# Even layer of a two-layer decoder step: six projections first, from split operands, then one run of attention steps

## The reference, cut to what matters

```python
proj = xn @ w_in                       # 1024 -> 6 x 512: q, k, v, g_a, u, g_b
z = q @ k.T / 8 + bias                 # per head, 8 heads of 64
lneg = where(mask, log_sigmoid(-z), 0)
tail = reverse_cumsum(lneg) - lneg     # stick-breaking weights
o_a = where(mask, exp(log_sigmoid(z) + tail), 0) @ v
o_b = pool_mix(u)                      # causal window means of 2, 4, 8, 16 and a small matmul
mixed = concat(o_a * silu(g_a), o_b * silu(g_b))
h = h + mixed @ w_out                  # k and v are outputs, too
```

## Time and profile before

| | |
|---|---|
| three runs, us | 2433.32, 2422.24, 2419.28 (median 2422.24) |
| the profiled execution, device time | 2424.9 us |
| its span in the trace | 2423.1 us |
| mean granted TensorE clock | 0.936 of 2.4 GHz |
| even layer up to the end of decode attention | 854.6 us of the span |

### The profile page before, as it was taken

The page is one execution under the profiler, slowest core; times in us unless marked ns, Lnnn a source line. Parts: engine busy times, 40 slices in busy tenths (PEclk is TensorE's granted clock), DMA queues, the critical chain, the costliest instruction groups (busy, mean ns, idle before and its releaser), DMA issues. The chain is left out here.

```text
span 2423.1 us, 28102 instructions
## 1 busy us (share of the span) xinstructions
PE 2126.3 (88%) x10945; PEld 1552.5 (64%) x10945; DVE 1072.6 (44%) x1840; ACT 650.8 (27%) x1116; POOL 94.4 (4%) x149
## 2 busy tenths in 40 slices
PE   4979797968967589899999979989999999967998
PEld 3646464644433234599999968559569569546885
DVE  4060606060222112274434345675675685656442
ACT  4150606060002111142222232132133133124321
POOL 0000000000000000000000000110110110110000
PEclk8989898989989699899999988899999999988999
DMA  3010101006026461258569432452453451756561
GB/s 119 14 40 6 47 0 53 0 24 190 21 85 200 134 166 63 41 107 130 143 155 188 133 136 83 170 182 93 170 193 112 177 191 61 262 191 205 156 178 31
DMA packets 180321, 281.81 MB, mean 116 GB/s; under 512 B 15363, under 2 KB 114695, under 8 KB 179098
## 3 DMA queue, kind: packets, MB, share of 16 engines
q1 hardware_dynamic: 151093, 183.12, 28.1%
q0 software_dynamic: 24256, 88.82, 10.2%
q10 hardware_dynamic: 4864, 8.39, 1.1%
HBM read 185.17 MB, written 95.31 MB: 116 GB/s over the span
## 5 line engine op out<-in xcount | busy, mean ns | idle before, releaser
L1297 PE MATMUL pre_ps<-x_xh,pre_wh 128*128 128x358 f32 (+1 forms) x792 | 260.3, 329 | 7.0 <-DVE pre_wl L1419 7.0
L1298 PE MATMUL pre_ps<-norm_xl,pre_wh 128*128 128x358 f32 (+1 forms) x792 | 259.1, 327 | 0.0
L1299 PE MATMUL pre_ps<-x_xh,pre_wl 128*128 128x358 f32 (+1 forms) x792 | 258.8, 327 | 0.0
L393 PE MATMUL attn_ps<-x_xnT,attn_w 128*128 128x512 f32 (+1 forms) x576 | 193.4, 498 | 9.5 <-DMA attn_w<-in_w_in_a 7.6
L393 PEld LDWEIGHTS attn_ps<-x_xnT,attn_w 128*128 128x128 f32 x576 | 97.0, 194 | 105.8 <-issue 98.1
L1297 PEld LDWEIGHTS pre_ps<-x_xh,pre_wh 128*128 128x128 f32 x792 | 149.8, 189 | 8.5 <-DVE pre_wl L1419 7.5
L1299 PEld LDWEIGHTS pre_ps<-x_xh,pre_wl 128*128 128x128 f32 x792 | 149.8, 189 | 0.0
L1298 PEld LDWEIGHTS pre_ps<-norm_xl,pre_wh 128*128 128x128 f32 x792 | 149.7, 189 | 0.0
L653 PE MATMUL pool_ps<-x_xnT,pool_w 128*128 128x512 f32 (+1 forms) x384 | 131.0, 504 | 13.9 <-DMA pool_w<-in_w_in_a 8.9
L1725 PE MATMUL head_ps<-head_cl,head_wh 128*128 128x358 f32 (+1 forms) x384 | 125.3, 326 | 0.0
L1724 PE MATMUL head_ps<-head_ch,head_wh 128*128 128x358 f32 (+1 forms) x384 | 125.0, 325 | 0.0
(11 more groups left out here) (388 smaller groups left out, 3795.6 us busy)
## 6 DMA issues: line engine op xcount, KB each, us to landing
head_Cs<-in_state_C POOLq DMA_DIRECT2D x32, 1024.0 KB, 5.8
out_C_s<-head_Cs POOLq DMA_DIRECT2D x32, 1024.0 KB, 4.8
x_xnT<-in_cache_sb_k SPq DMA_DIRECT2D x64, 256.0 KB, 3.0
all_w<-in_w_in_c SPq DMA_DIRECT2D x32, 512.0 KB, 10.7
x_dram<-low_low SPq DMA_DIRECT2D x16, 536.0 KB, 8.7
ca_dram<-low_low SPq DMA_DIRECT2D x16, 536.0 KB, 12.3
b_dram<-low_mid SPq DMA_DIRECT2D x16, 536.0 KB, 5.6
a_dram<-low_low SPq DMA_DIRECT2D x16, 536.0 KB, 6.1
```

The source lines that it names most:

```text
L393: last = pe.matmul(ps[:, bank + c, 0:c1 - c0], w[:, u, k, :], xnT[:, k, c0:c1], start=(k == 0), stop=(k == KD - 1))
L1297: pe.matmul(out, wh[:, t % 2, k, :], xh[:, k, c0:c1], start=(k == 0), stop=False)
L1298: pe.matmul(out, wh[:, t % 2, k, :], xl[:, k, c0:c1], start=False, stop=False)
L1299: last = pe.matmul(out, wl[:, t % 2, k, :], xh[:, k, c0:c1], start=False, stop=(k == KD - 1))
```

## The change

The even layer is cut in another way. `load_constants` also loads the first four token blocks, three weight blocks and the page table. `norm0_stage` leaves the normalised input as a high part `xe` and a low part `xl`. `even_input` makes all projections in one block: 24 weight blocks of 128 columns in the order of `TILES`, three products each, chunks of 368 columns. The means' small matmul (`y`) stands behind some of them (`TURNS`). v is made like k, features on partitions, and both are turned to token rows on PE (`turn_tokens`) through two PSUM banks (`side`). q, k and v of all heads stay in SBUF; the gates are written into `mixT` and later multiplied in place. `attention_steps` is one unrolled sequence of 36 groups, pair 0 rising from `t` = 0 to 8, pair 1 falling, and so on; the weights overwrite the sigmoid (`pos`), and the 16 columns of the longest rows beyond 1024 go through `tail`. SP loads the first four key units and the first sequence's values during these steps; values of the next three sequences are loaded within `decode_attention`.

```diff
+TILES = [("u", 0), ("u", 1), ("b", 0), ("u", 2), ("b", 1), ("u", 3), ("b", 2), ("b", 3)]
+TILES += [("v", c) for c in range(PAIRS)]
+TILES += [(kind, p) for p in range(PAIRS) for kind in "kqa"]
+AFTER = {("b", 0): 0, ("b", 1): 1, ("b", 2): 2, ("v", 0): 3}
...
+            def project(n):
+                t = tile_of(*TURNS[n])
+                pe.wait_ge(wl_done, t + 1)
+                wait_banks(n)
+                for c, (c0, c1) in enumerate(ECH):
+                    out = chunk(3 * (n % 2), c)
+                    for k in range(KD):
+                        pe.matmul(out, wh[:, t % 2, k, :], xh[:, k, c0:c1], start=(k == 0), stop=False)
+                        pe.matmul(out, wh[:, t % 2, k, :], xl[:, k, c0:c1], start=False, stop=False)
+                        last = pe.matmul(out, wl[:, t % 2, k, :], xh[:, k, c0:c1], start=False, stop=(k == KD - 1))
+                last.then_inc(full, 1)
...
+            def wait_side(r):
+                if r < 2:
+                    pe.wait_ge(rows_done, 2)
+                else:
+                    pe.wait_ge(side_done, r - 1)
...
+                    for c in range(PAIRS):
+                        if t == tile_of("v", c) + 1:
+                            for g in range(3):
+                                turn_tokens("v", c, g)
+                    if kind == "q":
+                        turn_tokens("k", p, 0)
+                        turn_tokens("k", p, 1)
+                    elif kind == "a":
+                        turn_tokens("k", p, 2)
...
+            def high(t):
+                act.wait_ge(w_in[t % WR], 16 * (t // WR + 1))
+                if t >= 2:
+                    act.wait_ge(full, turn_of(*TILES[t - 2]) + 1)
+                act.activation(wh[:, t % 2], w[:, t % WR], ACT.Copy).then_inc(wh_done, 1)
...
+            high(0)
+            for t in range(NF):
+                if t + 1 < NF:
+                    high(t + 1)
+                save(t)
...
+            for t, (kind, p) in enumerate(TILES):
+                if t + 1 < NF:
+                    low(t + 1)
...
+                for c in range(PAIRS):
+                    if t == tile_of("v", c) + 2:
+                        save_values(c)
...
+    GROUPS = [(p, t) for p in range(PAIRS) for t in (range(NT + 1) if p % 2 == 0 else range(NT, -1, -1))]
...
+            for n in range(KS):
+                load_pages(sp, table, cache_k, n // 2, PAGES // 2 * (n % 2), PAGES // 2, kp[:, n], k_in[n])
+            load_pages(sp, table, cache_v, 0, 0, PAGES, vp0, v_in0)
...
+            for u, (b, f) in enumerate(units[KS:], KS):
+                sp.wait_ge(z_full, u - KS + 1)
                 load_pages(sp, table, cache_k, b, HALF * f, HALF, kp[:, u % KS], k_in[u % KS])
+                if u % 2 == 0 and u < KS + 2 * (BG - 1):
+                    bb = (u - KS) // 2 + 1
+                    load_pages(sp, table, cache_v, bb, 0, PAGES, vp[bb], v_in[bb])
```

More of the change, by code:

```diff
@@ L150, in sem, with load_constants @@
         return self.sems[-1]
-def load_constants(nc, d, const, half, vcol, wcol, bias, prefT):
+def load_constants(nc, d, const, half, vcol, wcol, bias, biasN, prefT, x, x_in, w, w_in, table):
     with ExitStack() as ctx:
@@ L175, in _ @@
             sp.dma_start(prow[:, :], d["state_pool"].rearrange("l b r c -> (l b r) c")).then_inc(landed, 16)
+            sp.dma_start(table[:, :], d["page_table"].rearrange("(o b) n -> o (b n)", o=1)).then_inc(landed, 16)
+            for i in range(1, XS):
+                sp.dma_start(x[:, i, :], x_rows[i]).then_inc(x_in[i], 16)
+            for t in range(WR):
+                load_even(sp, d, w, w_in, t)
         @block.tensor
@@ L207, in norm_stage, with norm0_stage @@
+def norm0_stage(nc, d, const, x, work, x_in, xh, xl):
+    with ExitStack() as ctx:
+        s = Space(nc, ctx, "norm0")
+        sq, g, xn = work[:, 0, :], work[:, 1, :], work[:, 2:4, :]
         stat = s.sb("stat", [P, 2, 2])
         tp = s.ps("tp", [P, 2, 2, BANK])
[L209 to L212, removed]
@@ L229, in _ @@
         def _(pe):
-            def turn(i, q):
-                rows = P if i < NT else R8
+            for i in range(NT + 1):
+                rows = rows_of[i]
                 pe.wait_ge(xn_ready, i + 1)
@@ L304, in _ @@
                 if i >= 1:
[L305 to L318, removed]
-    full_blocks = [0] + [i + 1 for i in range(NT)]
[L320 to L326, removed]
+                    low(i - 1)
@@ L340, in attention_pairs @@
[L340 to L345, removed]
@@ L352, in _, with step, turns_before, tails_before @@
+        def step(n):
+            p, t = GROUPS[n // 2]
+            return p, t, n % 2
+        def turns_before(n):
+            return sum(turns[GROUPS[m // 2][1]] for m in range(n))
+        def tails_before(g):
+            return 2 * sum(1 for m in long_at if m < g)
         @block.sync
         def _(sp):
[L354 to L375, removed]
@@ L384, in _ @@
+            for j in range(2):
+                sp.wait_ge(kt_out[j], 16 * 3 * PAIRS // 2)
+            sp.wait_ge(v_out, 48)
         @block.tensor
         def _(pe):
-            def wait_proj(u):
-                pe.wait_ge(w_in[u], 16 * p + 16)
-            def project(u, bank):
-                wait_proj(u)
-                for c, (c0, c1) in enumerate(CHUNKS):
-                    for k in range(KD):
-                        last = pe.matmul(ps[:, bank + c, 0:c1 - c0], w[:, u, k, :], xnT[:, k, c0:c1], start=(k == 0), stop=(k == KD - 1))
-                last.then_inc(proj_full, 1)
@@ new lines, in tail @@
+            def tail(n):
+                p, t, j = step(n)
+                act.wait_ge(z_full, n + 1)
+                if n >= PN:
+                    act.wait_ge(t_full, turns_before(n - PN + 1))
+                c, z = slice(2 * BANK, keys[t]), ps[:, 6 + j, 0:META]
+                h = 2 * p + j
+                act.activation(pos[:, n % PN, c], z, ACT.Sigmoid, bias=biasB[:, h:h + 1])
+                act.activation(neg[:, n % PN, c], z, ACT.Sigmoid, bias=biasN[:, h:h + 1], scale=-1.0).then_inc(tail_done, 1)
@@ new lines, in sigmoids @@
+            def sigmoids(n):
+                p, t, j = step(n)
+                rows, L, h = META if t == 0 else P, min(keys[t], 2 * BANK), 2 * p + j
+                act.wait_ge(z_full, n + 1)
+                if n >= PN:
+                    act.wait_ge(t_full, turns_before(n - PN + 1))
+                z = ps[0:rows, 2 * j:2 * j + 2, :].rearrange("p a n -> p (a n)")[:, 0:L]
+                act.activation(pos[0:rows, n % PN, 0:L], z, ACT.Sigmoid, bias=biasB[0:rows, h:h + 1])
+                act.activation(neg[0:rows, n % PN, 0:L], z, ACT.Sigmoid, bias=biasN[0:rows, h:h + 1], scale=-1.0).then_inc(sig_done, 1)
@@ new lines, in copy_turned @@
+            def copy_turned(n):
+                p, t, j = step(n)
+                rows = META if t == 0 else P
+                if n >= 2:
+                    act.wait_ge(o_full, n - 1)
+                for m in range(turns[t]):
+                    r = turns_before(n) + m
+                    act.wait_ge(t_full, r + 1)
+                    k = min(4, full_blocks[t] - 4 * m)
+                    bank = ps[:, 4 + r % NG, :].rearrange("p (m r) -> p m r", r=P)
+                    if k > 0:
+                        last = act.activation(aT[:, j, 4 * m:4 * m + k, :], bank[:, 0:k, :], ACT.Copy)
+                    if m == turns[t] - 1:
+                        last = act.activation(aT[0:META, j, NT, 0:rows], bank[0:META, k, 0:rows], ACT.Copy)
+                    last.then_inc(t_done, 1)
@@ new lines, in output @@
+            def output(n):
+                p, t, j = step(n)
+                rows = META if t == 0 else P
+                c0 = PROMPT if t == 0 else META + P * (t - 1)
+                o = mixT[DA * j:DA * (j + 1), p, c0:c0 + rows]
+                dve.wait_ge(o_full, n + 1)
+                dve.tensor_tensor(o, ps[DA * j:DA * (j + 1), 6 + j, 0:rows], o, ALU.mult).then_inc(o_done, 1)
+            for g in range(G + 2):
+                early = g + 1 in long_at
+                for n in (2 * g - 4, 2 * g - 3):
+                    if early and g >= 2:
+                        output(n)
+                for n in (2 * g, 2 * g + 1):
+                    if g < G:
```

723 lines of the change are left out of this document (373 added, 350 removed).

## The result

The changed kernel takes 2322.68 us (median of 4 runs, 2318.91 to 2327.18) where the kernel before took 2420.92 in the runs beside it: a ratio of 0.9587, 95% interval 0.9554 to 0.962. The profiled execution took 2325.11 us with a span of 2323.3. The forecast was 2324.

A forecast was written before the change was run, and what follows sets the result against it. Projections were held PE-bound, attention steps a chain of waits. Start 52.0, projections 329.8, attention 210.5, decode 164.3 and rest 1568.5 sum to 2325.1, 98.0 below the 2423.1 span; 2422.2 less 98.0 gives about 2324 us, range 2298 to 2352.

The forecast's parts named there:

- Start: Kernel begin to first projection product: norm, splitting and first weight block were to take 52.0 us, bounds 49 to 55.
- Projections: Input block: PE-bound products of 24 weight blocks, plus turnings and waits, were to take 329.8 us, bounds 305 to 345.
- the four gaps: Input block: at each value block PE waits 3.2 us for DVE's copy before the last turning, 12.8 us in all.
- 1.0 a gap: Input block: assumed clock loss after each PE wait at a value block, between 0 and 2.0 us; 4.0 in all.
- Attention steps: Even layer's attention: one run of 36 groups was to take 210.5 us where 224 stood, bounds 164 to 224.
- each chain holds each size twice: Attention: two interleaved chains of steps; pair 0's 99.2 us, counted twice, gives 198.3 us for the run.
- Joining gives nothing: Rival: attention stays at 4 x 56.0 us, 13.5 more, kernel 2338 us; chance 0.17.
- Decode: Decode attention: SP's late key pages delay unit 9 and all behind by 12.1 us, to 164.3; bounds 152 to 168.
- page loads that keep up: Rival: decode attention stays at 152 us, kernel 2312 us; chance 0.12.
- The rest: Code behind decode attention, left unchanged, was to stay at 1568.5 us.
- Products at their length: Rival: each projection product waits for the one before, 0.331 us each, 284 us more, kernel 2608; chance 0.03.
- products that stand closer together: Rival: projection products about 156 ns apart, 19 us less, kernel 2305 us; chance 0.04.

## Why the prediction was right, point by point

- **Start: 52.0, measured 49.2.** Mis-sized. The first scaled block came at 19.5 us and not 18.0, since DVE waited 1.8 for the norm's weight; but a block then took 2.81 ((42.00 - 19.52)/8) and not 3.3. DVE waited 0.8 for ACT's high part once, not 0.35 in each round, and a round without a wait took 2.65 from start to start, where the forecast had added up lengths that overlap, to 2.95.
- **Projections: 329.8, measured 335.8.** The mechanism held, step by step: the 1728 products at 168.4 ns (166.9 forecast) add 2.6 us, the cold start cost 2.7 for 2.0, the four gaps 13.2 for 12.8, and the clock behind them 4 x 1.75 = 7.0 for 4.0; 0.7 less elsewhere. The forecast's 1.0 a gap lay between bounds of 0 and 2.0, and the truth near the upper one. Single gaps varied more: in the 32 gaps of the eight profiles that have them, three left the products 169.4 to 169.6 ns apart, and others cost up to 3.0 us. The sum didn't rest on what the split is worth against float32; that came out as 65 us.
- **Attention steps: 210.5, measured 206.7, for a wrong reason.** The step that failed is "in one run of 36 groups each chain holds each size twice", by which a rising and a falling pair cost the same 49.6 us and little but drains is saved, whatever the direction. In the changed kernel the two rising pairs took 44.9 and 45.8 from their first scores to the next pair's, the falling one between them 57.0. With the same sizes the steps took 206.7, 217.9 and 225.4 us as the order changed. Most of the 17 to 24 us won (against 224) comes from turning every second pair round within the run, so that longest meets longest, which the forecast had named as a point for *Joining gives nothing*. That rival holds nearly, for joining by itself (7.7 us or 2.4, where 13.5 was forecast). The pairs apart gave 225.6 for the 224 of 4 x 56.0. How DVE's waits grow out of each neighbour was not followed further.
- **Decode: 12.1 more, measured 13.3,** by the order on SP that the forecast went through; undone, 12.0 come back. The rival of page loads that keep up is excluded. The last link was another, though. The forecast had unit 7's scores end after 60.7 us and unit 9 wait for its keys until 73.5. Unit 7's scores ended after 62.5, unit 9 followed 11.6 later as it did before, and its keys, landed after 73.9, held nothing up.
- **The rest** is 2.4 us shorter, with the same code, which took 1552.4 to 1571.9 us in the other profiles.
- **Products at their length**, the other side, is excluded by 168.4 ns a product, and so are products that stand closer together. By the Trainium skill's page "TensorE: Matmul & The Clock Gate", section "Back-to-back issue gap", whose formula is given there for a single matmul by itself, 368 columns would be an estimated 155.8 ns apart; the measured 168.4 decides. The Trainium skill's figure on that page for the low clock, columns/1.2, gives an estimated 306.7 ns, and between 50 and 54 us, at a granted 0.50, the first block's products here were 306 to 307 ns apart: there the trace agrees.

The errors (-2.8, +6.0, -3.8, +1.2 and -2.4) nearly cancel: part of the near hit is luck, the more so as the rest alone varies by more than 10 us from profile to profile.

## What to carry to other kernels

When a block of projections is bound by PE, the price is the distance between starts in a full stretch, and every other engine's order has to be read for one question: what stands ahead of the piece that PE waits for? Two edits that only reorder one engine's list, copies ahead of a low part and value pages into an idle stretch of SP, took about 30 us more off a kernel that had already won 98. Where groups of different size run in a chain, try equal neighbours together at the turning points; here joining runs alone gave little.

## What was not expected of the hardware

- A gap of 3.3 us in a stream of matmuls was followed by 4.7 us at a mean granted clock of 0.64, between the levels of 1.2 and 2.4 GHz, so that a gap cost 1.75 us more than itself, on average over four. It did not always: behind 3 of 32 such gaps the products stayed 169.4 to 169.6 ns apart. Gaps of 0.4 to 0.5 us at the same places left the clock at 1.00 in all three profiles that have them.
- A float32 block of 1104 columns cost 14.85 us in chunks of 368 columns in place of 15.6 in chunks of 512, 512 and 80. By the column the products of 80 columns took 1.40 ns, those of 368 and 512 columns 0.84.
- The same code gave 170.3 us of decode at a granted 0.75 and 176.5 at 0.71, and 200.4 to 206.7 us of attention steps. Stages where PE often waits vary by 3 to 4% from run to run; what sets the clock there was not tried.
